# Other orders for the attention stage's steps, and own programs for its last two steps and the seam

## The reference

```
q, k, v = split(h @ w_qkv, 3)            # 8 heads; q and k of a head: 2 components of 64; v: 128
s = einsum('bqhcd,bkhcd->bhcqk', q, k) / 8 + bias[t5_bucket(key - query)]
p = softmax(where(chunk(key) <= chunk(query), s, -inf))
w = p[:, :, 0] - lam * p[:, :, 1]
o = rmsnorm(w @ v, subln_g) * (1 - lam_init)
return o @ w_o
```

## Time and profile before

| | |
|---|---|
| median of three runs | 2055.14 us |
| the profiled execution's own time | 2058.21 us |
| its span, first to last instruction | 2056.4 us |
| TensorE matmul busy | 2007.3 us, 98% |
| VectorE busy | 1569.8 us, 76% |
| ScalarE busy | 896.7 us, 44% |
| GpSimd busy | 224.7 us, 11% |
| mean granted TensorE clock | 0.985 |

### The profile page before, as it was taken

The page is one execution under the profiler, slowest core; times in us unless marked ns, Lnnn a source line. Parts: engine busy times, 40 slices in busy tenths (PEclk is TensorE's granted clock), DMA queues, the critical chain, the costliest instruction groups (busy, mean ns, idle before and its releaser), DMA issues.

```text
span 2056.4 us, 40288 instructions
## 1 busy us (share of the span) xinstructions
PE 2007.3 (98%) x15908; PEld 1944.4 (95%) x15908; DVE 1569.8 (76%) x2223; ACT 896.7 (44%) x1415; POOL 224.7 (11%) x337
## 2 busy tenths in 40 slices
PE   7999999999998999999999999999999999999998
PEld 7999999989887899999999999999999988999997
DVE  6797778767775779777968896687888757977794
ACT  6443334345554534333438764333343334433342
POOL 5000000422212200000051111000000151000000
PEclk8999999999998999999999999999999989999999
DMA  5423333332111223333336541223342422233332
GB/s 164 135 83 103 93 111 89 97 105 62 54 52 44 78 83 103 98 86 102 98 108 139 130 107 52 83 83 103 102 122 66 126 67 82 83 102 102 102 103 93
DMA packets 304528, 195.22 MB, mean 95 GB/s; under 512 B 7354, under 2 KB 297147, under 8 KB 304148
## 3 DMA queue, kind: packets, MB, share of 16 engines
q1 hardware_dynamic: 298972, 175.08, 29.8%
q0 software_dynamic: 4240, 14.09, 3.2%
q10 hardware_dynamic: 1192, 4.34, 0.5%
HBM read 179.45 MB, written 6.44 MB: 90 GB/s over the span
## 4 chain that ended last, share of the span: by engine, by line
PE 81%; DVE 9%; ACT 4%; issue 3%; DVEq 1%; POOLq 1%; DMA 0%; SPq 0%; ACTq 0%; POOL 0%
PE ps L924 38%; PE ps L1188 34%; PE ps L1041 2%; PE ps L1299 2%; PE ps L982 1%; DVE scores L2558 1%; ACT scores L1896 1%; PE ps L1025 1%; DVE w_lo L2149 1%; PE ps L1403 1%; DVE weights L2580 1%; POOLq L803 1%; POOLq L800 1%; DVE wt_lo L2594 0%; DVE y_lo L2155 0%
## 5 line engine op out<-in xcount | busy, mean ns | idle before, releaser
L1188 PE MATMUL ps<-t_lo,y_hi 128*128 128x264 f32 (+1 forms) x1008 | 285.7, 283 | 0.0
L1188 PE MATMUL ps<-t_lo,w_hi 128*128 128x264 f32 (+1 forms) x1008 | 285.7, 283 | 0.0
L1188 PE MATMUL ps<-t_hi,w_lo 128*128 128x264 f32 (+1 forms) x1008 | 285.4, 283 | 0.0
L1188 PE MATMUL ps<-t_hi,y_lo 128*128 128x264 f32 (+1 forms) x1008 | 285.3, 283 | 0.0
L1188 PE MATMUL ps<-t_hi,w_hi 128*128 128x264 f32 (+1 forms) x1008 | 285.1, 283 | 0.1
L1188 PE MATMUL ps<-t_hi,y_hi 128*128 128x264 f32 (+1 forms) x1008 | 284.8, 283 | 0.0
L1799 ACT ACTIVATE w_hi<-w_raw 128x1024 fp32r<-128x1024 f32 (+1 forms) x108 | 127.8, 1201 | 330.3 <-PE ps L924 194.1
L924 PE MATMUL ps<-hid_hi,w_hi 128*128 128x264 f32 (+1 forms) x1184 | 265.2, 296 | 0.4 <-DVE hid_lo L2444 0.4
L924 PE MATMUL ps<-hid_lo,w_hi 128*128 128x264 f32 (+1 forms) x1184 | 264.7, 296 | 0.0
L924 PE MATMUL ps<-hid_hi,w_lo 128*128 128x264 f32 (+1 forms) x1184 | 264.1, 295 | 0.0
L924 PE MATMUL ps<-y_hi,w_hi 128*128 128x264 f32 (+1 forms) x1088 | 246.3, 303 | 3.5 <-DVE q L2668 1.7
(11 more groups left out here) (342 smaller groups left out, 4384.0 us busy)
## 6 DMA issues: line engine op xcount, KB each, us to landing
w_raw<-in_ffn_w_gate SPq DMA_DIRECT2D x88, 512.0 KB, 5.0
w_raw<-in_ffn_w_up SPq DMA_DIRECT2D x88, 512.0 KB, 4.7
w_raw<-in_ffn_w_down SPq DMA_DIRECT2D x70, 512.0 KB, 4.3
w_raw<-in_ffn_w_down SPq DMA_DIRECT2D x24, 384.0 KB, 4.4
w_raw<-in_attn_w_qkv SPq DMA_DIRECT2D x16, 512.0 KB, 3.7
w_raw<-in_conv_w_in SPq DMA_DIRECT2D x16, 512.0 KB, 4.0
w_lo<-w_raw POOLq DMA_DIRECT2D x16, 512.0 KB, 5.1
w_raw<-in_attn_w_qkv SPq DMA_DIRECT2D x16, 256.0 KB, 2.8
```

What stands on the lines that cost most here:

```text
L1188: mm = pe.matmul(ps[:, bank, 0:hw], w[:, at:at + P], b[:, t, k, 0:hw], start=k == 0 and n == 0, stop=k == 3 and n == 2)
```

## The change

Sums, operands and results are as before. What is moved:

- VectorE, each step: `split_lo` of the next head's k tile moves from the end of step h to step h + 1, behind `row_maxima` of tile 0; `o_lo(h - 3)` moves from the front to behind it. `combine` of tile 2 goes ahead of the low half of w01. The low half of w2 goes ahead of the low halves of q and k, and the reading of v becomes the last instruction. `om_lo` goes ahead of the low half of w2.
- ScalarE, each step: `weights_hi` of w2 goes ahead of the high halves of q and k; the small copies of q, k and v for the meta tokens move to the front of the next step.
- Group scores: `score_meta` goes right behind `score` of tile 1, into other columns of the same two banks, without its own wait for the fourth tile's maxima. Maxima, exponentials and weights of the group have buffers of their own and come behind tile 1's. VectorE's maxima of tile 1 wait for both scores.
- Step 8 gets own programs on TensorE and VectorE (`attention_last_scores`). TensorE turns w3 first, then runs the early blocks in other portions: 5, 1, 2, 2, 2, 2, 4, 2, 4, 3 around the same operations (27 instead of 28). VectorE has `add_early` in other places, and `split_lo` of the next output tile behind the first maxima.
- The end: early blocks 3, 3, 5, 10 instead of 4, 3, 5, 8; `om_lo` and `o_lo` ahead of `add_early(6)`.
- The seam: late blocks 6 and 7 use banks 2 and 0 instead of 4 and 6. `y_lo` of blocks 2 to 7 comes behind all eight `add_late`, and `head_by_blocks` of this layer waits for all eight blocks of `h` instead of four.

```diff
-LATE_BANKS = (4, 6, 2, 0, 4, 6, 4, 6)
+LATE_BANKS = (4, 6, 2, 0, 4, 6, 2, 0)
...
-                        pe.wait_ge(s.h_ready, NB * hn + 4)
+                        pe.wait_ge(s.h_ready, NB * hn + (NB if r == R_FFN1 else 4))
...
             def score_meta(h):
 
                 cols = group_cols(h)
-                pe.wait_ge(s.scores_read, tile_number(h, QT))
                 pe.wait_ge(s.qk_meta_copied, h + 1)
...
+            def attention_last_scores():
+
+                h, h1, h2 = HEADS, HEADS - 1, HEADS - 2
+                turn_last_weights(h2)
+                some_early(5)
+                pe.wait_ge(s.qk_ready, h1 * 2 + 2)
+                score(h1, 0, 0)
+                some_early(1)
+                pe.wait_ge(s.scores_read, tile_number(h1, 0) + 1)
+                pe.wait_ge(s.turned_lo, turn_number(h, "w3") + 1)
+                weights_times_v(h2)
+                pe.wait_ge(s.qkv_read, h1 * 3 + 3)
+                banks67_free(h, "v")
+                turn_v(h1)
+                some_early(2)
+                pe.wait_ge(s.o_copied, h2 + 1)
+                score(h1, 0, 1)
+                score_meta(h1)
+                some_early(2)
+                banks67_free(h, "sums")
+                o_sums(h2)
+                some_early(2)
+                score(h1, 0, 2)
+                some_early(2)
+                banks67_free(h, "w01")
+                turn_weights(h1, (0, 1)).then_inc(s.turned, 1)
+                some_early(4)
+                pe.wait_ge(s.part_added, 2)
+                score(h1, 0, 3)
+                some_early(2)
+                banks67_free(h, "o")
+                spread_factors(h2)
+                some_early(4)
+                banks67_free(h, "w2")
+                turn_weights(h1, (2,)).then_inc(s.turned, 1)
+                some_early(3)
...
+            def meta_maxima(h):
+
+                rows = group_cols(h)
+                n = rows.stop - rows.start
+                for c in range(2):
+                    dve.tensor_tensor_reduce(out=m.meta_scores[rows, c, 0:n], in0=ps[rows, 4 + c, META + 3 * P:META + 3 * P + n],
...
+            def attention_step(h, par, mid, old):
...
+                if old:
+                    weights_lo(h, "w3", 3, 3, h2 if group_of(h2) else None)
+                if mid:
+                    row_maxima(h1, par, 0)
+                    split_lo(t0 + 1, h, 4, SLOT)
+                if not (isinstance(h, int) and h <= 2):
+                    o_lo(h - 3)
+                split_lo(t0 + 2, h, 4, 512)
...
+                split_lo(t0 + 4, h, 4, SLOT)
+                read_projection(h, par, 1, m.k, 1.0)
                 if mid:
+                    dve.wait_ge(s.turned, turn_number(h, "w01") + 1)
+                    combine(h1, 2)
                     weights_lo(h, "w01", 0, 1)
-                    combine(h1, 2)
                     row_maxima(h1, par, 3)
+                if old:
                     norm_rows(h2, h)
                 if mid:
                     combine(h1, 3)
+                if old and group_of(h2):
+                    om_lo(h2)
                 if mid:
                     weights_lo(h, "w2", 2, 2)
+                for c, x in enumerate((m.q, m.k)):
+                    dve.wait_ge(s.qk_hi_ready, h * 2 + (c + 1))
+                    dve.tensor_tensor(m.qk_lo[:, c, :], x[:, :], m.qk_hi[:, c, :].bitcast(F32), ALU.subtract)\
+                       .then_inc(s.qk_ready, 1)
+                read_projection(h, par, 2, m.v, 1.0)
...
+            def attention_last_scores():
+
+                h, h1, h2 = HEADS, HEADS - 1, HEADS - 2
+                out0 = first["attn_out"]
+                weights_lo(h, "w3", 3, 3)
+                row_maxima(h1, 0, 0)
+                split_lo(out0 + 1, 0, 0, EARLY * P)
+                o_lo(h - 3)
+                combine(h1, 0)
+                split_lo(out0 + 2, 0, 0, EARLY * P)
+                add_early(0)
+                v_lo(h, h1)
+                row_maxima(h1, 0, 1)
+                meta_maxima(h1)
+                guess_factors(h2, h)
+                combine(h1, 1)
+                combine(h1, QT)
+                add_early(1)
+                row_maxima(h1, 0, 2)
+                split_lo(out0 + 3, 0, 0, EARLY * P)
+                dve.wait_ge(s.turned, turn_number(h, "w01") + 1)
+                combine(h1, 2)
+                weights_lo(h, "w01", 0, 1)
+                add_early(2)
+                row_maxima(h1, 0, 3)
+                norm_rows(h2, h)
+                split_lo(out0 + 4, 0, 0, EARLY * P)
+                combine(h1, 3)
+                weights_lo(h, "w2", 2, 2)
+                add_early(3)
+                split_lo(out0 + 5, 0, 0, EARLY * P)
...
             for d in range(NB):
                 add_late(d)
-                if d > 0:
-                    y_lo(d - 1, Y_FFN1, ROW_FFN + 1, 0, TOK)
-                if d in (2, 4):
-                    split_lo(first["up1"] + d // 2 - 1, 0, 0, SLOT)
-            y_lo(NB - 1, Y_FFN1, ROW_FFN + 1, 0, TOK)
+                if d in (1, 4):
+                    y_lo(d // 3, Y_FFN1, ROW_FFN + 1, 0, TOK)
+                if d in (3, 6):
+                    split_lo(first["up1"] + d // 3 - 1, 0, 0, SLOT)
+            for d in range(2, NB):
+                y_lo(d, Y_FFN1, ROW_FFN + 1, 0, TOK)
```

More of the change, by code:

```diff
@@ L301, in __init__ @@
         self.row_ratio = row_maxima[:, 6:7]
+        meta_maxima = new("meta_maxima", [P, 8])
+        self.meta_max, self.neg_meta_max = (meta_maxima[:, 2 * n:2 * n + 2] for n in range(2))
+        self.meta_ratio = meta_maxima[:, 4:5]
+        self.meta_scores = self.scores[:, :, META + 3 * P:META + 3 * P + 6 * META]
         self.o_x = new("o_x", [P, 5])
@@ L494, in tile_number @@
 def tile_number(h, j):
-    return h * QT + (j + sum(isinstance(h, int) and g < h for g in GROUPS))
+    if isinstance(h, int):
+        order = (0, 1, QT, 2, 3) if h in GROUPS else (0, 1, 2, 3)
+        return h * QT + sum(g < h for g in GROUPS) + order.index(j)
+    return h * QT + j
 def group_of(h):
@@ L2010, in attention_step @@
                     om_hi(h2)
+                if mid:
+                    weights_hi(h, "w2", 2, 2)
                 if proj:
-                    wait(act, s.scores_done, tile_number(h1, QT - 1) + 1)
+                    if not (isinstance(h, int) and h == 0):
+                        act.wait_ge(s.scores_done, tile_number(h1, QT - 1) + 1)
                     for c, x in enumerate((m.q, m.k)):
@@ L2670, in read_projection, with v_lo @@
                    .then_inc(s.qkv_read, 1)
[L2672 removed]
+            def v_lo(h, h1):
+                dve.wait_ge(s.turned_hi, split_number(h, "v") + 1)
+                dve.tensor_tensor(m.v_lo[:, :, :], ps[:, 7, :].rearrange("p (j e) -> p j e", j=QT),
+                                  m.v_hi[:, 1:, :].bitcast(F32), ALU.subtract)
+                if group_of(h1):
+                    dve.tensor_tensor(m.vm_lo[:, :], ps[:, 6, P:2 * P], m.vm_hi[:, :].bitcast(F32), ALU.subtract)
+                dve.tensor_tensor(m.v_hi[2 * STRIP:STACK, 0, :], ps[0:META, 6, 0:P],
+                                  m.v_hi[0:META, 0, :].bitcast(F32), ALU.subtract).then_inc(s.turned_lo, 1)
+            def attention_step(h, par, mid, old):
                 h1, h2 = h - 1, h - 2
                 t0 = first["attn"]
[L2675 to L2676 removed]
                 if old:
@@ new lines, in attention_end @@
+            def attention_end():
+                h, h2 = HEADS + 1, HEADS - 1
+                out0 = first["attn_out"]
+                o_lo(h - 3)
+                weights_lo(h, "w3", 3, 3, h2)
+                for c in (6, 7):
+                    split_lo(out0 + c, 0, 0, EARLY * P)
+                add_early(4)
+                guess_factors(h2, h)
+                add_early(5)
+                split_lo(out0 + NB, 0, 0, 512)
+                norm_rows(h2, h)
+                om_lo(h2)
+                o_lo(h2)
+                add_early(6)
+                split_lo(out0 + NB + 1, 0, 0, 512)
+                add_early(7)
+                for c in range(2, LATE_TILES):
+                    split_lo(out0 + NB + c, 0, 0, 512)
```

189 lines of the change are left out of this document (63 added, 126 removed).

## The result

The changed kernel takes 2039.47 us as the median of four runs (2039.27 to 2041.72), the kernel before beside it 2054.86 us (2053.34 to 2057.99). The ratio is 0.9926, 95% interval 0.9908 to 0.9943: faster by 15.4 us where 14.3 were forecast. The profiled execution took 2041.72 us, its span is 2040.0 us.

What follows compares the result with a forecast made beforehand. TensorE, busy 98% of the span, was taken as the bound, with about 28 us of waits and lower clock in reach. Terms 7.35 + 0.85 + 4.35 - 0.25 + 2.0 = 14.3 us gave 2041 us, range 2034.5 to 2048.5.

Steps and rivals of the forecast that it cites:

- The eight steps: Attention steps: TensorE's wait for the turned weights' low half goes in five steps, 7.35 us gained with the clock.
- the group scores: Group scores beside the second tile's: waits of 0.85 and 0.2 us go, 0.2 for k comes; net 0.85 us in step 6.
- forecast of 27.4 us for the step: Sign that the prediction is right: the steady attention step, 28.34 us before, becomes 27.4 us.
- the low half first: VectorE, end of a step: w2's low half directly behind the weights is ready at 545.1 instead of 546.10, removing TensorE's wait.
- the 0.9 us in which it waited for ScalarE: VectorE, each step: the third tile's weights, ahead of tiles 0 and 1's low half, fill this wait; no gain counted.
- The moved split: The 1.23 us weight split and o_lo behind the next step's first row maxima are hidden in VectorE's waits: cost 0.
- The slower rival: Split and o_lo behind the first row maxima are not hidden, each of seven steps 1.75 us longer: 2062 us, chance 0.05.
- The last step: Last step with scores: idle falls from 9.3 to 7.15 us, clock loss from 5.7 to 3.5; 4.35 us gained.
- 0.47 us wait before the weighted sum: Attention stage: TensorE's wait of the weighted sum for the first row maxima, idle 0.47 us once, stays unchanged.
- End step and seam: End step loses 0.25 us with three covering blocks; at the seam 2.93 us of waits become 0.95, 2.0 us gained.
- GpSimd's squares: Rival at the seam: adds of squares slowed by y_lo leave 2.4 us idle at the token sums; 2043.5 us, chance 0.10.
- the last step opens up: Rival: o_lo or add_early come earlier than walked, or the clock stays; 6.0 us more gained, 2035 us, chance 0.14.

Runs made afterwards that it cites:

- x2: Changed kernel with the low halves of q and k, and v's reading, again ahead of the third tile's turned weights' low half: 2040.55 us, ratio 0.9908.
- x4: Changed kernel with both step orders put back (q, k, v before w2's low half; w01's low half before the third tile's weights): 2049.23 us, ratio 0.9958.
- x5: Changed kernel with the next head's weight-tile split back at the end of a step and o_lo first in the next: 2039.92 us, ratio 0.9925.
- x6: Changed kernel with the step after the last head and the end step in their old order, group scores still moved: 2044.31 us, ratio 0.9946.
- x1: Changed kernel with the seam alone put back (old late banks, y_lo between the adds, waiting for four blocks of h): 2039.29 us, ratio 0.990.
- x8: Changed kernel with a narrower wait for k's reading and a rearranged step after the last head (early blocks, o_lo, third part sum): 2031.46 us, ratio 0.9879.
- x7: Changed kernel with the first early output-projection block waiting for k's reading alone, not also for v's: 2038.05 us, ratio 0.9915.
- x9: The changed kernel itself, timed again beside the version with the rearranged last step: 2040.87 us (2034.32 to 2042.58), ratio 0.9915.
- x10: The version with the narrower wait and rearranged last step, timed again beside the changed kernel: 2031.18 us (2029.30 to 2031.51), ratio 0.9869.

## Why the prediction was right, and where its terms were off

The forecast was 2041 us and 2039.47 came out; 14.3 us of gain were forecast, and 15.4 lie between the medians. In the traces of before and after alone, the stage is 17.8 us shorter, 3.5 us more than the terms add up to, and each part of it (the steps, the last step, the end with the seam) came out larger than forecast. That the number came closer than its terms is luck. In these two traces 1.6 us of the stage's gain are lost again by a step 0 that begins later. Step by step:

- **The eight steps.** Forecast 7.35 us and 0.85 for the group scores, 8.2 in all (0.2 of it for a wait in step 7 that lies behind the landmark); measured 177.7 - 167.8 = 9.9. All five waits went, no other took their place but 0.19 us for k in step 6 (forecast 0.2), and the clock is full from 440 to 620. The mechanism is right; the size is off because a wait costs more than the trace prints. The printed 0.95 us of the earlier trace rows begin where the last block matmul is modelled to end, 0.28 us after its start (545.77). Without a wait the next one starts 0.12 us after it, as at 541.20 above. So from the start of the last block matmul to the turn are 1.23 us before and 0.12 after, 1.11 us for a printed 0.95; and the turn's first four transposes take 0.06 us less when they run on without a stop (541.20 to 541.63, before 547.00 to 547.49). The steady step went from 28.34 to 27.15 us: 1.19 for a printed 0.95. Five such waits make 1.1 us of the missing 1.7, the wait before the group's scores some 0.2 more. The turn of step 7 was late too, though no wait is printed: it started at 604.46, 0.4 us behind the start of the last block matmul, where 0.12 is the pitch. The forecast of 27.4 us for the step was 0.25 us too long for the same reason.
- **Which edit does it.** The prediction credited the low half first alone, and moved the third tile's weights into "the 0.9 us in which it waited for ScalarE" at no gain. x2 shows that this second edit alone takes away almost the whole gap too, and x4 that the gap needs both orders back. The sum was not hurt by it, since both were made, but that is luck as far as the cause goes: the prediction gave to one edit what either of two brings.
- **The moved split.** Costed at 0, with 0.85 us of VectorE's idle time left before `v_lo`; 0.86 are left. The slower rival did not happen. x5 shows the other side of it, which the prediction missed: the end of a step has no room for the split any more.
- **The last step.** Forecast 4.35 us, idle 7.15 in four waits and 3.5 of clock. Measured idle is 7.26 in the same four (2.02, 1.25, 2.35, 1.64), and the clock cost 3.4 by the estimate above. The stretch is 6.35 us shorter, 0.74 of them the moved block: 5.6 us. So the walk through the new program was right, and the 1.3 us more lie in what the kernel before lost. Its printed waits in this stretch are 9.92 us and not 9.3: the 0.47 us wait before the weighted sum, which stood in the forecast as unchanged, went, and the 0.16 us before the group's weights was counted with the group. With 7.26 against 7.15 behind, that is 0.5 us. Its clock (0.83, 0.61 and 0.88 in the 10 us from 630, 650 and 660) lost up to 6.8 us, part of it while TensorE stood idle, against the 5.7 that was taken. This, and the unprinted share of three waits fewer, some 0.2 us each, cover the other 0.8; how they share it stays open.
- **End step and seam.** Forecast -0.25 and +2.0. The end step's wait is 0.38 us, and by x6 it costs 0.6; the seam's is 1.10 where 0.95 stood, and x1 prices the seam at 2.1. Both together are 47.5 - 46.0 + 0.74 for the block = 2.2 us, where 1.75 stood. The 0.7 us between 2.1 - 0.6 and 2.2 lies in the end step: with before's portions x6 needs 8.30 us from its turn to the sums of the squares (664.66 to 672.96), before needed 8.99 (676.71 to 685.70), with no printed wait in either.
- **GpSimd's squares.** The rule of the Trainium skill ("SBUF — State Buffer", "Who interferes with whom") was weighed as a rival. The adds did slow down, by the median from 1.53 to 1.88 us, and of 4.3 us between the end of the last add and the token sums 1.7 are left. No wait came of it. The price was misread. The 2.33 us that the rival took for an add beside `y_lo` stand in the trace of before behind a weight split, which also reads two operands from SBUF; the same holds for the other add of 2.32 us:

```profile
704.34 1.21 DVE L2149 TENSOR_TENSOR w_lo<-w_raw,w_hi 128x1024 fp32r<-128x1024 f32 x1
...
704.41 2.33 POOL L802 TENSOR_TENSOR sumsq<-sumsq,o_square 128x528 f32<-128x528 f32 x1 [0.56 <-issue]
...
707.28 1.31 POOL L802 TENSOR_TENSOR sumsq<-sumsq,o_square 128x528 f32<-128x528 f32 x1 [0.54 <-issue]
...
707.84 1.31 DVE L2155 SCALAR_TENSOR_TENSOR y_lo<-h,vec,y_hi 128x528 fp32r<-128x528 f32 x1
```

Nor is an add of 1.31 us one that runs alone: the one at 707.28 has a `y_lo` beside it, and it is this `y_lo` that takes longer, 1.31 us instead of 0.76. In the changed kernel the three adds beside the six `y_lo` take 1.88 to 1.90 us, those of 1.94 and 2.06 start during a weight split, and those of 1.32 and 1.33 have little but additions to `h` beside them, which read one operand from PSUM. So the trace agrees with the rule and not with the price: at 1.9 us six adds need 2.2 us more than at 1.53, an estimate, and 2.4 were to spare.

- **Rival "the last step opens up"**, 2035 us: it did not with this program, which leaves four waits; x8 is that case, made by a few small edits, and at 2031.5 us it goes further.

## What to carry to other kernels

When the end of a loop's body is late on one engine, look for how much it is late, not for the one instruction to move: here two orders each removed the gap of 0.95 us alone, and only putting both back showed what they were worth. Price a wait in a matmul stream by the pitch of the loop with and without it, not by the printed idle time. And once the steady steps are free of waits, walk the steps at the loop's end with the same care: their waits were longer, brought the lower clock with them, and gave another 8 to 10 us for a few moved lines and one narrower wait.

## What the runs showed of the hardware

The clock behind a wait is not a fixed price. With the same program and nearly the same waits the granted clock fell twice in the last step of one execution (0.83 from 620 to 630 and from 650 to 660 us) and once in that of another (0.83 from 630 to 640), and that stretch of the kernel took 65.9 and 64.1 us. A wait of 1.25 us less in x7 went with 1.4 to 2.8 us between the medians and 2.9 to 4.7 us of the last step between the traces, most of it clock. Why the clock falls in one execution and not in the next was not tried.

That the scatter of the whole time comes from these waits is not shown. It was 8.3 us with them (x9) and 2.2 without (x10), but the changed kernel's first four runs lie within 2.5 us, and x4 and x6, with longer waits in the last step, within 2.9 and 2.3 us. The clock of the first 60 us and of the stretches at 1200 and 1640 us moves it as well, as x1 shows.

VectorE and GpSimd slowed each other where both read two operands from SBUF, and in these rows the instruction that started first kept its time. In the trace of before the add at 707.28 kept its 1.31 us, while the `y_lo` that started 0.56 us later took 1.31 instead of 0.76; the weight split at 704.34 kept its 1.21 us, and the add that started 0.07 us later took 2.33.
